# Stick-breaking heads ahead of the forget-gate heads in the attention of a two-layer block

## The reference

```python
for i in range(DEPTH_2):                       # 2 layers
    h = x @ w_in[i]
    (fq, fk, fv, ff_logit, sq, sk, sv, dq, dk, dv, iq, ik, iw, g) = split_cols(h)
    o_fox = fox_attention(fq, fk, fv, log_f)           # 6 heads
    o_sb  = stick_breaking_attention(sq, sk, sv)       # 5 heads
    o_dsa = dsa_attention(dq, dk, dv, iq, ik, iw)      # 5 heads, one key and value head
    gates = sigmoid(g.reshape(b, s, 3, D_MODEL))
    merged = gates[..0] * (o_fox @ w_up_fox) + gates[..1] * (o_sb @ w_up_sb) + gates[..2] * (o_dsa @ w_up_dsa)
    x = layer_norm(ALPHA * x + merged @ w_out, ...)
    ffn = square(relu(x @ w_ff_in)) @ w_ff_out
    x = layer_norm(ALPHA * x + ffn + sigmoid(x @ w_ple_gate) * (p @ w_ple), ...)
```

## Time and profile before

| | |
|---|---|
| median of 3 runs | 1881.11 us (1878.58 to 1883.79) |
| profiled execution, its own time | 1878.79 us |
| its span, first to last instruction | 1877.0 us |
| TensorE matmul busy | 1684.2 us, 90% |
| VectorE busy | 877.6 us, 47% |
| ScalarE busy | 462.8 us, 25% |
| mean granted TensorE clock | 0.913 of full speed |
| attention heads, layer 1 and layer 2 | about 847 to 980 us, 1428 to 1561 us |

### The profile page before, as it was taken

The page is one execution under the profiler, slowest core; times in us unless marked ns, Lnnn a source line. Parts: engine busy times, 40 slices in busy tenths (PEclk is TensorE's granted clock), DMA queues, the critical chain, the costliest instruction groups (busy, mean ns, idle before and its releaser), DMA issues. The chain is left out here.

```text
span 1877.0 us, 22240 instructions
## 1 busy us (share of the span) xinstructions
PE 1684.2 (90%) x8995; PEld 1320.9 (70%) x8995; DVE 877.6 (47%) x1367; ACT 462.8 (25%) x779; POOL 36.8 (2%) x59
## 2 busy tenths in 40 slices
PE   4997989997799987989999899994998999799995
PEld 2555879456499976768786699963776877499972
DVE  0634975334355540028654555534007664555536
ACT  2102232111244421002320344411002221244420
POOL 0002010000000000000000000000000000000000
PEclk8987989665899997999999899996999999899997
DMA  9421110331345406331232455504432322445420
GB/s 360 155 90 45 46 46 2 108 117 46 134 146 196 150 0 220 129 135 50 85 135 90 179 182 194 197 8 148 158 135 70 111 90 90 179 177 182 182 87 22
DMA packets 102162, 228.80 MB, mean 122 GB/s; under 512 B 5441, under 2 KB 13761, under 8 KB 101313
## 3 DMA queue, kind: packets, MB, share of 16 engines
q1 hardware_dynamic: 99056, 219.80, 32.9%
q10 hardware_dynamic: 3024, 7.90, 1.1%
HBM read 226.64 MB, written 1.05 MB: 121 GB/s over the span
## 5 line engine op out<-in xcount | busy, mean ns | idle before, releaser
L814 PE MATMUL psum<-xT,ring 128*128 128x256 f32 (+1 forms) x1504 | 338.0, 386 | 10.4 <-issue 9.6
L814 PEld LDWEIGHTS psum<-xT,ring 128*128 128x128 f32 (+1 forms) x1504 | 274.1, 186 | 63.8 <-issue 15.2
L586 PE MATMUL psum<-channels_rounded,work_rounded 128*128 128x256 f32 x1536 | 284.6, 286 | 2.7 <-DVE work_rounded L654 2.7
L623 DVE TENSOR_TENSOR work_rounded<-ring,work_rounded 128x1024 fp32r<-128x1024 f32 x192 | 222.4, 1220 | 103.1 <-ACT work_rounded L614 102.9
L597 PE MATMUL psum<-work_rounded 128*128 128x512 f32 x1152 | 265.7, 390 | 0.0
L586 PEld LDWEIGHTS psum<-channels_rounded,work_rounded 128*128 128x128 f32 x1536 | 244.7, 195 | 5.0 <-issue 4.1
L597 PEld LDWEIGHTS psum<-work_rounded 128*128 128x128 f32 x1152 | 214.7, 188 | 43.6
L614 ACT ACTIVATE work_rounded<-ring 128x1024 fp32r<-128x1024 f32 x192 | 187.6, 1049 | 175.2 <-PE psum L597 108.3
L586 PE MATMUL psum<-work_rounded 128*128 128x256 f32 x768 | 219.3, 286 | 0.0
L586 PEld LDWEIGHTS psum<-work_rounded 128*128 128x128 f32 x768 | 149.4, 195 | 0.8
L1216 DVE RECIPROCAL work<-work 128x256 f32<-128x256 f32 x48 | 84.1, 1753 | 1.6
(11 more groups left out here) (353 smaller groups left out, 1966.8 us busy)
## 6 DMA issues: line engine op xcount, KB each, us to landing
ring<-in_w_in SPq DMA_DIRECT2D x22, 2048.0 KB, 8.1
ring<-in_w_ff SPq DMA_DIRECT2D x16, 2048.0 KB, 8.0
ring<-in_w_ff_in SPq DMA_DIRECT2D x16, 2048.0 KB, 7.7
ring<-in_w_ff_out SPq DMA_DIRECT2D x16, 2048.0 KB, 7.8
ring<-in_w_mod SPq DMA_DIRECT2D x12, 2048.0 KB, 8.0
ring<-in_w_out SPq DMA_DIRECT2D x6, 2048.0 KB, 8.0
ring<-in_w_up SPq DMA_DIRECT2D x4, 2048.0 KB, 9.0
ring<-in_w_ple_gate SPq DMA_DIRECT2D x4, 2048.0 KB, 8.0
```

The costliest lines, as they stand in the source:

```text
L586: mm = pe.matmul(psum[:, 4 + 2 * half + q, i * SEQ:(i + 1) * SEQ], w1[pw][:, k, m * P:(m + 1) * P], y[py][:, k, :], start=((k, n) == (0, 0 ...
L623: dve.tensor_tensor(parts.low[i % 2][:, at], ring[:, SLOT * (n % RING) + 1024 * c: SLOT * (n % RING) + 1024 * (c + 1)], exact(parts.high[i ...
L814: mm = pe.matmul(ps[base:base + m, at:at + SEQ], unit[:, k, col:col + m], yT8[:, k, :], start=(k == 0), stop=(k == KC - 1))
```

## The change

The five sb heads stand first in `HEADS`, then the six fox heads, then the five dsa heads as before. The wait for `sk12` moves from the first fox head to the first sb head. One line is added, so all later lines of the file move by one (L967 becomes L968, L1280 becomes L1281).

```diff
-HEADS = [("fox", h) for h in range(6)] + [("sb", h) for h in range(5)] + [("dsa", h) for h in range(5)]
+HEADS = [("sb", h) for h in range(5)] + [("fox", h) for h in range(6)] + [("dsa", h) for h in range(5)]
...
                             elif kind == "S":
+                                if name == "sb0":
+                                    w.after("sk12")
                                 if name == "fox0":
                                     w.after("cumT")
-                                    w.after("sk12")
                                 if name == "dsa0":
```

## The result

The changed kernel took 1886.53 us (median of 20 runs, 1880.75 to 1894.53), the kernel before 1879.26 us (20 runs, 1872.56 to 1886.8). The ratio is 1.0041, interval 1.0029 to 1.0054: slower by 0.4%. The forecast was 1889.0 us. A second set of runs gave 1.0038 (1.0018 to 1.0057). The profiled execution has a span of 1883.3 us, 6.3 more than before.

The account below looks back on a forecast made before the run. TensorE, busy 90% of the span, was taken to bound the kernel. New waits of 5.6 us, 0 for the other steps and 3.4 us of clock falls gave 9.0 us, so 1889 us, range 1883 to 1893.

Parts of the forecast that it names:

- Part 1, the V of sb4: V of sb4, behind fox0's two top-k rounds on VectorE, waits 2.8 us per layer, 5.6 us in two.
- What would have shown it in the profile: TensorE's V of sb4 shows about 2.8 us of idle time, twice in the trace; under 2 us refutes the forecast.
- Part 2, the rest: Other steps of the new head order: sb waits unchanged, fox steps without wait, no load late; 0 us, -0.6 to +0.6.
- Part 3, the clock: Granted clock falls behind each new wait of V of sb4, 1.7 us each, 3.4 us in all; old falls stay.
- The sum: Whole kernel: 5.6 + 0 + 3.4 = 9.0 us slower, forecast 1889 us.
- The one without a new fall: Behind V of sb4 no new clock fall, old ones stay: 5.6 us alone, 1885.5 us; chance 22%.
- The one with more falls: Waits of sb0 and sb2 both bring a clock fall: 9.0 + 2.4 = 11.4 us, 1891.3 us; chance 16%.
- The escape from the low clock: Stick-breaking stretch: old clock falls go, no new ones come, waits alone cost 3.2 us, 1883.1 us; chance 15%.
- the faster: Rounds at V of sb4 are hidden after all and old clock falls go: about 1877.5 us; chance 4%.
- the staying-behind case: VectorE stays late after sb4, so fox1 or fox2 waits again, another 2 x 2.8 us: 1894.6 us; chance 7%.

Follow-up runs that it names:

- The equal pair 0.9922 and 0.9923: Old order with VectorE's sigmoids behind the weights, and new order with that plus top-k rounds one head later, each against the kernel before: 0.9922 and 0.9923.

## Why the prediction was right, and where it was off

- **Part 1, the V of sb4: right.** 7.09 us from the scores to V against 1.12 + 2.87 + 3.09 = 7.08 by the earlier trace rows; the step is 2.82 us longer (2.8 forecast). The place was shown from three sides: the rounds away from it, the rounds put there in the old order, half of the rounds. What would have shown it in the profile was put badly: 2.8 us of idle time holds only if TensorE comes to the wait at the high clock. It came at the low one, so the trace shows 1.00 and 1.17 us.
- **Part 2, the rest: right.** sb0, sb1 and sb2 are no worse, the fox steps have no wait of TensorE, no load is late. The equal pair 0.9922 and 0.9923 shows this better than the trace.
- **Part 3, the clock: right in kind, partly wrong in its account.** A spell follows V of sb4 in all four layers profiled of the changed kernel, and TensorE kept busy there doesn't have it. Its price was 1.7 to 1.8 us in three of them, as forecast, and 3.4 in the fourth. That the old spells stay was right in number and wrong in place: the one behind sb2 is gone, one behind sb0 has come (-1.18, +1.03). The order alone doesn't set that: the old order with extra rounds has it behind sb0 in its first layer, the new order with the rounds elsewhere behind sb2 in its first. A spell that I didn't forecast stands behind sb3. It cost only 0.1 to 0.3 us, since it lay on work ahead of a wait.
- **The sum:** 9.0 us forecast, 6.3 between the two profiles, 7.3 between the medians, 8.1 in the second set. The base of the forecast, 1880 us, was also 0.7 above the median of 20 runs. The term that was too large is the clock's: 3.4 us of it were right, but 1.0 us a layer came back behind the heads, where the spell on the transposes didn't recur. That looks like chance of the single execution: the old order with extra rounds has no spell there either, and the new order with the wait filled has one in its first layer. It should have been left to the range.
  The Trainium skill ("TensorE: Matmul & The Clock Gate", "What's actually happening") puts the ramp penalty at under 1% of a typical kernel span and warns against fitting to a specific cold count. In size the trace agrees: two spells of 1.7 us are 0.2% of this span. To leave the clock out on that ground is my reading of it, and would have given 5.6. The first set of medians lies halfway between that and my sum, the second nearer to mine.
- **The rivals.** The one without a new fall was nearer in time (1885.5, against 1886.53 measured and 1889.0 forecast). That is luck: its mechanism is refuted, since the fall came in every layer, and what brought the time down lay behind the heads. The one with more falls was nearest in the spells (three among the heads, not two), but not in time, and the third stood behind sb3 and not where it had it. The escape from the low clock, the faster and the staying-behind case didn't come.

## What to carry to other kernels

Look at what an in-order engine does between two parts of a chain that another engine waits for. Work that fits beside one family of heads can stand on the path of another: here two top-k rounds, free behind a softmax head's maxima, cost 2.8 us ahead of a stick-breaking head's sum. When a reordering pairs the items of two pipelines differently, check the step in which the families meet. And the work between them that nobody waits for, as the sigmoids here, belongs behind the operation that is waited for, whatever the order.

## What the runs showed of the hardware

The granted clock fell also behind a wait of 0.48 us, when TensorE went on with V of 128 x 64 products and fox scores with 64 and 6 rows (894 us in the changed kernel, again in its second profile). Behind V of sb4 it fell after waits of 1.00 to 1.29 us ahead of the same products, and not when four 128 x 256 products filled the wait. It fell also with no wait near: at 934 to 939 us in the second profile of the changed kernel TensorE's last wait lay 32 us back. A low clock ahead of a wait cost little. The step of sb4 lasted 10.13 and 10.26 us in one profile of the changed kernel and 10.38 and 10.13 in the other, with some 1.7 us of slow work in it. An estimate for the high clock is 7.22 + 2.82 = 10.04 us: the step with the rounds elsewhere, and what the extra rounds added in the old order.
